# Head norms' root moved behind the last exponential, three modulation steps moved from one product to another, and one small sum put in another PSUM bank

## The reference, cut to what matters

```python
mod = jax.nn.silu(c) @ w_ada[l] + b_ada[l]
sh1, sc1, ga1, sh2, sc2, ga2 = jnp.split(mod, N_MOD, axis=-1)
h = modulate(rms_norm(x, g_norm1[l]), sh1, sc1)
qa, ka, va, oa, gates, qb, kb, vb = jnp.split(h @ w_in[l], IN_SPLITS, axis=-1)
h_a = mlstm_bidirectional(q_a, k_a, v_a, g_a)
h_a = h_a * lax.rsqrt(jnp.mean(h_a * h_a, axis=-1, keepdims=True) + EPS)
h_a = from_heads(h_a) * g_head_a[l] * jax.nn.sigmoid(oa)
h_b = from_heads(neighborhood_attention(to_heads(qb), to_heads(kb), to_heads(vb), rpb[l]))
mixed = jnp.concatenate([h_a, h_b], axis=-1) @ w_out[l]
x = x + ga1[:, None, :] * mixed
```

## Time and profile before

| what | value |
|---|---|
| median of 3 runs | 2580.28 us (2579.51 to 2580.51) |
| the profiled execution, its time and span | 2586.97 us, span 2585.2 us |
| TensorE busy | 2546.0 us, 98% of the span |
| VectorE, ScalarE, GpSimd busy | 1686.8, 1295.0, 213.1 us |
| DMA | 591.55 MB, mean 229 GB/s |
| 64 us beside the neighbours (356 to 420 us) | TensorE 60.9, VectorE 52.5, ScalarE 38.4, GpSimd 31.8 us busy |

### The profile page before, as it was taken

One profiled execution on the slowest core, in us unless ns is written; L12 is line 12 of the kernel. 1 busy time (PEld: TensorE's weight loads), 2 busy tenths in 40 slices (PEclk: granted clock), 3 DMA queues, 4 the chain that ended last, 5 costly groups with the idle time before them and its releaser, 6 DMA issues.

```text
span 2585.2 us, 31168 instructions
## 1 busy us (share of the span) xinstructions
PE 2546.0 (98%) x11494; PEld 2069.8 (80%) x11494; DVE 1686.8 (65%) x1897; ACT 1295.0 (50%) x1613; POOL 213.1 (8%) x263
## 2 busy tenths in 40 slices
PE   7999999999999999999999999999999999999998
PEld 3887878878888888888888777888888888888887
DVE  4969879978777766655565678556655555555454
ACT  2454456445555555444544567454555555554443
POOL 0021133100000000000100135001000000000000
PEclk9999999999999999999999999999999999999999
DMA  9979978978888787666677644656666666666664
GB/s 371 410 255 343 307 253 269 341 220 270 275 261 268 218 219 211 188 205 205 192 228 219 179 139 139 187 192 206 193 215 207 205 201 207 199 213 201 192 194 154
DMA packets 374417, 591.55 MB, mean 229 GB/s; under 512 B 120980, under 2 KB 121356, under 8 KB 373804
## 3 DMA queue, kind: packets, MB, share of 16 engines
q1 hardware_dynamic: 348368, 518.59, 64.0%
q0 software_dynamic: 18928, 69.39, 7.9%
q10 hardware_dynamic: 7020, 2.26, 0.6%
HBM read 563.94 MB, written 2.10 MB: 219 GB/s over the span
## 4 chain that ended last, share of the span: by engine, by line
PE 87%; DVE 5%; DMA 3%; issue 2%; ACT 1%; SPq 1%; POOL 0%; DVEq 0%; ACTq 0%
PE gp L1626 27%; PE gp L1628 27%; PE gp L1627 27%; DVE w_lo L2175 2%; DVE ada_sum L2302 1%; DMA ada_ring<-in_w_ada_dram 1%; DMA proj<-in_w_ada_dram 1%; DMA raw<-in_w_in_dram 1%; DMA raw<-in_w_up_dram 1%; ACT w_hi L969 1%; PE tp L2077 0%; PE tp L1935 0%; PE tp L1786 0%; PE tp L1925 0%; PE tp L1711 0%
## 5 line engine op out<-in xcount | busy, mean ns | idle before, releaser
L2175 DVE TENSOR_TENSOR w_lo<-raw,w_hi 128x1024 fp32r<-128x1024 f32 x872 | 1072.9, 1235 | 754.8 <-ACT w_hi L969 752.1
L969 ACT CAST w_hi<-raw 128x1024 fp32r<-128x1024 f32 x872 | 911.3, 1050 | 988.9 <-PE gp L1628 801.8
L1626 PE MATMUL gp<-w_hi,h_hi 128*128 128x512 f32 x2636 | 1037.4, 394 | 6.7 <-DVE w_lo L2175 6.6
L1628 PE MATMUL gp<-w_hi,h_lo 128*128 128x512 f32 x2636 | 1026.4, 389 | 0.0
L1627 PE MATMUL gp<-w_lo,h_hi 128*128 128x512 f32 x2636 | 1026.3, 389 | 0.0
L1626 PEld LDWEIGHTS gp<-w_hi,h_hi 128*128 128x128 f32 x2636 | 495.1, 188 | 119.5 <-DVE w_lo L2175 10.3
L1628 PEld LDWEIGHTS gp<-w_hi,h_lo 128*128 128x128 f32 x2636 | 495.0, 188 | 104.3
L1627 PEld LDWEIGHTS gp<-w_lo,h_hi 128*128 128x128 f32 x2636 | 495.3, 188 | 100.6 <-issue 0.2
L1626 PE MATMUL gp<-w_hi,a_hi 128*128 128x512 f32 x704 | 274.3, 390 | 0.0
L1627 PE MATMUL gp<-w_lo,a_hi 128*128 128x512 f32 x704 | 273.9, 389 | 0.0
L1628 PE MATMUL gp<-w_hi,a_lo 128*128 128x512 f32 x704 | 273.9, 389 | 0.0
(11 more groups left out here) (339 smaller groups left out, 1439.9 us busy)
## 6 DMA issues: line engine op xcount, KB each, us to landing
raw<-in_w_in_dram SPq DMA_DIRECT2D x248, 512.0 KB, 4.5
raw<-in_w_up_dram SPq DMA_DIRECT2D x176, 512.0 KB, 4.6
raw<-in_w_ffn_in_dram SPq DMA_DIRECT2D x176, 512.0 KB, 4.4
ada_ring<-in_w_ada_dram POOLq DMA_DIRECT2D x128, 512.0 KB, 5.9
raw<-in_w_down_dram SPq DMA_DIRECT2D x88, 512.0 KB, 4.5
raw<-in_w_ffn_down_dram SPq DMA_DIRECT2D x88, 512.0 KB, 4.5
proj<-in_w_ada_dram SPq DMA_DIRECT2D x64, 512.0 KB, 9.3
raw<-in_w_out_dram SPq DMA_DIRECT2D x64, 512.0 KB, 5.2
```

The costliest lines, as they stand in the source:

```text
L969: nc.scalar.copy(w_hi[:, s], raw[:, s]).then_inc(hi_ready, 1)
L1626: mm(o, hi[:, kt0 + kt, ps], w_hi[:, s, k, :], start=n == 0, stop=False)
L1628: return mm(o, lo[:, kt0 + kt, ps], w_hi[:, s, k, :], start=False, stop=n == g.kts - 1)
L2175: V.tensor_tensor(w_lo[:, s], raw[:, s], w_hi[:, s].bitcast(F32), ALU.subtract).then_inc(lo_ready, 1)
```

## The change

The root goes from ScalarE's step 1 of in-o into `neighbours` at k = HB+1 = 9 (its step 12), without the second table load. The additions (and their loads) of steps 4, 5 and 6 of in-a1 leave that list, and in-o's list gains steps 1, 2 and 3; the sum over k that each addition makes, and their order, stay the same. GpSimd's loads follow: before `window(0)` it issues the loads up to in-o's step 3 in the new list (two gate loads in place of five), before `window(4)` four loads in place of two, and in all later places the load that stood one place earlier. Here `n0` is 2 where it was 5. In the front the columns of the second quarter are made in bank 1 of `tp`, VectorE reads them there, and TensorE transposes pair 3 without the wait for that read; the filler product is doubled and stands behind the transposes.

```diff
--- before.py
+++ after.py
@@ -539,10 +539,10 @@
             return 2 if b in (10, 16, 22) else 1
         assert 4 + sum(halves_adds(b) for b in range(HALF_B)) == 2 * DT
         OPEN_ADA = (36, 37, 38, 39)
-        IN_A1_ADA = [q for q in range(24) if q not in (1, 2, 3)]
+        IN_A1_ADA = [q for q in range(24) if q not in (1, 2, 3, 4, 5, 6)]
         IN_A_ADA = len(OPEN_ADA) + len(IN_A1_ADA)
         IN_B_ADA = list(range(1, 32))
-        IN_O_ADA = list(range(4, 16))
+        IN_O_ADA = list(range(1, 16))
         IN_B_END = IN_A_ADA + len(IN_B_ADA)
         assert IN_B_END + len(IN_O_ADA) == PART2C
         OUT_ADA = list(range(1, 9)) + list(range(10, 30))
@@ -890,11 +890,12 @@
                 ada_gate(n)
             for n in range(HB):
                 if n == 4:
-                    ada_gate(n0)
+                    for m in range(3):
+                        ada_gate(n0 + m)
                 if n >= 4:
-                    ada_gate(n0 + n - 3)
+                    ada_gate(n0 + n - 1)
                 window(n)
-            for n in range(n0 + HB - 3, 2 * (DT - K1)):
+            for n in range(n0 + HB - 1, 2 * (DT - K1)):
                 ada_gate(n)
 
             pool.wait_ge(na_max, HB)
@@ -1207,10 +1208,6 @@
                     nc.scalar.copy(sel_one[:, :, :], sel[:, :, :]).then_inc(sel_ready, 1)
                 if k in BIAS_AT:
                     bias(BIAS_AT.index(k))
-                if k == ML0 + HA * ML_H + 1:
-                    act.wait_ge(ml_ms, 1)
-                    nc.scalar.activation(hcol[:, 2, :], hcol[:, 1, :], ACT.Sqrt).then_inc(ml_rms, 1)
-                    act.preload_act_table_set("natural_log_exp_and_others")
                 h, part = (k - ML0) // ML_H, (k - ML0) % ML_H
                 if k < ML0 or h >= HA:
                     return
@@ -1240,7 +1237,6 @@
             stream(g_in_a1, no_drain, each=at(g_in_a1, mlstm, k1=ML0), nxt=g_in_b, unrolled=True)
             stream(g_in_b, drain_proj(g_in_b, proj, QB0 + 2 * CW), each=at(g_in_b, mlstm, ML_B), nxt=g_in_o,
                    unrolled=True)
-            heads_end = ML0 + HA * ML_H
 
 
             def neighbours(k):
@@ -1273,6 +1269,9 @@
                         "p t (r c) -> p t r c", c=GW), by_row(tp[:, 3, 0:S])[:, :, ::-1].rearrange(
                         "p (t r) c -> p t r c", t=ST)).then_inc(na_stored, 1)
 
+                if k == HB + 1:
+                    act.wait_ge(ml_ms, 1)
+                    nc.scalar.activation(hcol[:, 2, :], hcol[:, 1, :], ACT.Sqrt).then_inc(ml_rms, 1)
                 if k == HB + 4:
                     na_high()
 
@@ -1303,8 +1302,6 @@
             na_at = at(g_in_o, neighbours)
 
             def in_o_each(i, e, j, first):
-                if first and j == 1:
-                    mlstm(heads_end + 1)
                 na_at(i, e, j, first)
             stream(g_in_o, drain_o, each=in_o_each, nxt=g_out, unrolled=True)
 
@@ -1775,7 +1772,7 @@
 
             def quarter_bias(qd):
 
-                mm(tp[:, 3, 0:HK1].rearrange("p (u k) -> p u k", u=2), brow,
+                mm(tp[:, 3 - 2 * qd, 0:HK1].rearrange("p (u k) -> p u k", u=2), brow,
                    ident[0:2 * DT, 0:2 * DT].rearrange("p (u k) -> p u k", u=2)[:, :, qd * HK1 // 2:(qd + 1) * HK1 // 2],
                    start=True, stop=False)
 
@@ -1797,7 +1794,7 @@
             def quarter_columns(qd):
                 pe.wait_ge(row_ready, qd + 1)
                 for q in range(4):
-                    last = mm(tp[:, 3, q:q + 5:4], half_rows[0:64, q * P:(q + 1) * P], ident[0:64, 0:33:32],
+                    last = mm(tp[:, 3 - 2 * qd, q:q + 5:4], half_rows[0:64, q * P:(q + 1) * P], ident[0:64, 0:33:32],
                               start=False, stop=q == 3)
                 last.then_inc(mod_sum, 1)
 
@@ -1864,9 +1861,8 @@
                     pe.wait_ge(row_ready, 2)
                     quarter_bias(1)
                     quarter_columns(1)
-                    keep_busy(1, tp[:, 0, 0:P])
-                    pe.wait_ge(mod_ready, 2)
                     transpose_x(0, (3,), 0)
+                    keep_busy(2, tp[:, 0, 0:P])
                 if b == QUARTER_B + 1:
                     transpose_x(0, (4, 5, 6), 0)
             stream(g_first, h_hi, h_lo, 0, h_pairs(HB_NORM0), each=first_each, by_part=HB_NORM0)
@@ -2321,11 +2317,11 @@
                     ins = V.scalar_tensor_tensor(dst, ring, col, dst, ALU.mult, ALU.add)
                 ins.then_inc(done, 1)
 
-            def mod_part(a, b, done):
+            def mod_part(a, b, done, bank=3):
                 n = b - a
                 dve.wait_ge(mod_sum, done)
-                V.tensor_copy(mod[:, 0, a:b], tp[:, 3, 0:n])
-                V.scalar_tensor_tensor(mod[:, 1, a:b], tp[:, 3, n:2 * n], 1.0,
+                V.tensor_copy(mod[:, 0, a:b], tp[:, bank, 0:n])
+                V.scalar_tensor_tensor(mod[:, 1, a:b], tp[:, bank, n:2 * n], 1.0,
                                        vcol[:, 0, VC["g1"] + a:VC["g1"] + b],
                                        ALU.add, ALU.mult).then_inc(mod_ready, 1)
 
@@ -2366,7 +2362,7 @@
             split(*FRONT[3])
             for n in range(HK1 + 2, DT):
                 weigh(n, 1)
-            mod_part(HK1 // 2, HK1, 2)
+            mod_part(HK1 // 2, HK1, 2, 1)
             split(*FRONT[4])
             low_half(2)
             split(*FRONT[5])
```

## The result

The changed kernel takes 2588.74 us (median of 8, 2584.97 to 2595.53), the kernel before in the same comparison 2580.40 us (median of 8, 2578.25 to 2583.76): ratio 1.0031, interval 1.0020 to 1.0042, so it is slower by 8 us (5 to 11). A second comparison gave 1.0029 (1.0020 to 1.0038). The profiled execution took 2590.24 us, its span is 2588.5.

What follows compares the result with a forecast made beforehand. TensorE, holding 87% of the chain that ended last, was taken as the bound. The sum 0 - 2.0 (in-a1) + 5.95 (in-o) + 1.0 (clock) = +4.95 us gave a median of 2585.2 us, range 2576.8 to 2588.8.

Steps and rivals of the forecast that it cites:

- mechanism: In in-o, loads queued behind four mask windows land late; VectorE's addition of step 4 waits 7 us, TensorE stands at step 3.
- Root: In-o's head: moving the square root removes the 2.68 us stall, alone giving back 4.4 us; its new place costs 0.
- in-a1: Removing three modulation steps there clears four small TensorE stalls: -2.0 us, bounds -1.2 and -2.1.
- Windows' end: In-o: GpSimd's first four mask windows, slowed beside VectorE's additions, end at 374.0 us, bounds 370.7 and 374.4.
- Landing: In-o: the load for step 4 lands 6.7 us after issue, with bias in flight, at 380.7 (bounds 374.5 and 382.5).
- Chain behind the addition: In-o: TensorE's transposes of step 3 still follow the start of step 4's addition by 5.81 us, so in-o ends 5.95 later.
- Clock: In-o: TensorE's clock falls after the long pause, adding 1.0 us, bounds 0 and 1.7.
- in-o as a whole: The stage in-o ends 5.95 us later than before, plus 1.0 us for the lower clock.
- The base: Profiled execution, 2586.97 us, lay 6.7 above the median 2580.28; the same forecast difference was put on both.
- (a): Rival, short wait in in-o: load lands at 375 to 378, total -1.5 to +2, about 2580.5; chance 0.23.
- (b): Rival, no wait in in-o: step 4's data are there before 374.75, total -3.2, 2577; chance 0.14.
- (c): Rival, trailing loads: those behind windows 4 to 6 also late, each in-o step pays 1 to 2 us, +8 to +14; chance 0.11.

Runs made afterwards that it cites:

- steps_only: Only the three modulation steps moved from in-a1 to in-o, against the kernel before; root and front as before: 2588.13 us, ratio 1.0033.
- loads_early: Changed kernel, but GpSimd issues the loads of in-o's steps 4 to 6 behind window 0: 2577.39 us, ratio 0.9985 to the kernel before.
- bias_later: Changed kernel, but ScalarE issues the bias of heads 4 to 7 one step later each: 2585.86 us, ratio 1.0023 to the kernel before.

## Why the prediction was right, and where its sizes were off

The forecast was +4.95 us (2585.2), it is +8.3 (5 to 11), inside the range, and slower as forecast. But it is inside by luck: 2588.74 against an upper end of 2588.8, and just past the +8 to which the forecast's own terms reach. The point was 3 us short, and the chance of slower by more than 0.2%, 0.37, was too small for what it had found. What is right is the mechanism, shown by steps_only and loads_early.

- **Root.** Right in kind: no stall at the head, no cost at the new place. 4.4 us were taken from one execution with the low clock; 3.4 (1 to 6) timed.
- **in-a1.** -2.0 forecast, -2.9 and -3.05 (steps alone -2.99). The stalls of 198.90, 203.11 and 236.70 are gone, as said; the fourth did not go (0.39 before, 0.56 now). So the stalls account for 1.5 us. The column also has open, the product ahead: 0.4, 0.5 and 0.8 us of the gain lie ahead of split 40, in-a1's first, where TensorE's wait of 0.32 us at 167.41 is gone as well (it is absent from the second profile of before, too). In in-a1 alone the gain is 2.2 to 2.5 us, and the same program differs from itself by up to 0.7 there. So the term was about right; what the gain has beyond the stalls is not explained.
- **Windows' end.** Forecast 374.0, that is 15.4 us after the last load; it is 15.9. The count of one selection per addition was right: in GpSimd's rows above, those from 360.48 to 363.39 take 1.25 to 1.38 us each.
- **Landing.** Forecast 6.7 us, measured 7.7 and 9.0: undersized by 1.0 and 2.3 us. The prediction took the lower end of its range since fewer bias loads stood near; bias_later shows that the bias alone is 3 to 4 us of it. What the other loads in flight (the three went out at once, behind a block of weights) add is not shown.
- **Chain behind the addition.** The prediction kept the 5.81 us from the addition of step 4 to the transposes of step 3. In the profile of before, the scores ahead of these (379.14) did not wait for VectorE, they came when TensorE was through with the work before them, 4.39 us after the addition's start. In the changed kernel, where TensorE does wait, they come 2.82 us after it (380.54 against 377.72), and in its second profile 2.81. So this step was wrong by 1.6 us, to the long side. The row of before:

```profile
379.14 1.03 PE L1990 MATMUL tp<-proj 128*128 128x256 f32 x4
```

- **Clock.** Forecast 1.0 us behind the long pause, bounds 0 and 1.7. From scores to next transposes the step takes 7.96 us in the changed kernel, 7.17 in its second profile and 6.95 with the steps alone, against 4.92 elsewhere: 3.0, 2.3 and 2.0 us. All three lie above the upper bound; this is the most undersized term of the sum.
- **in-o as a whole.** Forecast 5.95 + 1.0 = 6.95; by stage 7.34 and 8.73 against the same profile. That 7.34 comes so near is luck: the chain was taken 1.6 us too long and the clock's price 2 us too low, and the two errors nearly cancel. Counted from TensorE's first transposes of in-o, the scores of step 3 start 4.9 us later than before (6.9 in the second profile), the clock adds 3.0 (2.3), and 0.6 us that TensorE lost in the same step of the kernel before are gone.
- **The base.** The prediction set the difference on the profiled execution and the median alike. It did not ask whether the extra 6.7 us of that execution lay in the stages that it was reading. They did, in part: up to 2.3 us of its in-o. Against the mean of such executions the root's gain is 1.3 us smaller and in-o's loss 1.3 us larger than against that one.
- **Rivals.** (a) and (b) fall: the data landed at 377.7 and VectorE waited 9.8 us. (c), trailing loads: in both profiles of the changed kernel VectorE never waits for the ring after step 4, and a later wait is for TensorE (1.67 us at 390.00), so they did not trail, though the time is nearly that which (c) gave at its lower end (+8).

The port rule of the Trainium skill (SBUF — State Buffer, Terms) is borne out once more by the selections at 1.25 to 1.38 us beside the additions. The drain that the Trainium skill (ScalarE: Activation LUTs, What ACT_TABLE_LOAD costs) adds to each switch is not seen in this kernel either: in the changed kernel the root's table load ends at 418.23 and its activation starts at 418.25.

```profile
416.95 1.28 ACT L1274 ACT_TABLE_LOAD   x1
418.25 0.21 ACT L1274 ACTIVATE hcol<-hcol 128x8 f32<-128x8 f32 x1
```

## What to carry to other kernels

Moving an operation into an engine's idle time moves its load too: read the queue that issues the load, and ask what now stands ahead of the next one. Here three additions of 1.28 us nearly fitted the gap, and the loads behind four windows of masks made VectorE wait 9.8 us; the same additions with the loads sent behind the first window are faster than before. And before a stall of one profile is priced, a second profile of the same kernel tells which part of it recurs.

## What the runs showed of the hardware

- The low clock behind a stall of about 2 us is not a fixed price: the same program ran the block's first product behind it at 0.99 us or at 0.58 from one execution to another. It was low behind stalls of 2.68, 2.55 and 2.65 us and full behind 1.86 and 2.15 us (2.65 and 2.15 in variants).
- Behind TensorE's stalls of 7.03, 8.36 and 8.74 us the low clock cost 2.0, 2.3 and 3.0 us.
- A load of 512 KB issued while two loads of 96 KB in small packets are in flight landed in 7.7 and 9.0 us, without them in 4.9, each time with two more loads of its own kind behind it. Issued one by one, 1.2 us apart and before the bias loads, each landed in 5.6 to 5.8.
- Work on TensorE near 66 us at the full clock in place of the lower one (0.85 us less on four products) brought nothing: the next late block of weights took it back within 16 us.
